# Attention of a two-block layer kernel: the values are multiplied with the probabilities as the stationary operand

## The chip, the cores and the metric

One Trainium2 chip, one of its cores. The metric is the device time of one launch in microseconds, median of several runs, lower is better.

## The reference, cut to what matters

Two layers run one after the other on 512 tokens of width 1024, all in float32. The change touches only the attention of the second layer and the norm behind it. There, eight heads "A" have three branches each (selected keys `slc`, a window `win`, compressed keys `cmp`), and eight heads "B" (`mla`) have one. With at most 16 blocks of 64 keys and 512 tokens the selection and the window cover every earlier key, so `slc`, `win` and `mla` are causal attention over 512 keys with value rows of width 64; `cmp` has 31 keys.

```python
o_c = einsum('bgrqn,bngd->bqgrd', masked_softmax(s_c, ...), vc)
o_s = einsum(...masked_softmax(s_s, mask_s)..., vs)
o_w = einsum(...masked_softmax(s_w, mask_w)..., vw)
o_a = gate0 * o_c + gate1 * o_s + gate2 * o_w          # 512 tokens x 8 heads x 64
o_b = einsum('bhqs,bshd->bqhd', masked_softmax(s), v)  # 512 tokens x 8 heads x 64
mixed = concat([rmsnorm(o_a, out_gain_a), rmsnorm(o_b, out_gain_b)]) @ w_out
h = x + mixed
return h + peer_ffn(rmsnorm(h, norm2_gain), ...)
```

## The kernel before, in words

Every engine has a program written out by hand, and semaphores join them. TensorE (PE) is the engine that nearly all of the work goes to.

The attention is a list of 104 steps, `STEPS`. A step is one branch of one head and one tile `qt` of 128 queries; it has `(qt+1)*128` keys. A head A has nine steps (`slc` 0, 1, `cmp`, `slc` 2, 3, `win` 0 to 3), so rounds 0 to 71 are the A heads; each B head has four, rounds 72 to 103. All engines go through the rounds `u` in the same order:

- PE, round `u`: `scores` of step `u+4` (L1076 to L1098, into PSUM bank `(u+4) % 4`), some products with values from `VALUES_AT[u]` (`output`, L1134; `cmp`: L1127), and `turn` of step `u` (L1108), which transposes the tiles of probabilities into PSUM bank `4 + u % 2`.
- VectorE (DVE), round `u`: `tops` of step `u` (row maximum of the scores, L2218) and `biases` (L2229); two rounds late `inverses` (L2242) and `shares` (L2257, L2259), which multiplies the whole tile of probabilities by one over its sum and by the gate. `turn` of the step waits for `shares`.
- ScalarE (ACT), round `u`: `probs` (Exp with its row sum, L1585), and `turned` of step `u-4`, which copies the transposed tiles out of PSUM (L1600). A head whose values are done is copied out as 64 rows (features) by 512 tokens (L1623) into `oall`.

In `output` the values (128 keys by 128 columns, of which a head uses 64) are stationary and the transposed probabilities move: for key tile `kt` there are `(4-kt)*128` columns. A float32 product is two instructions on PE. All branches of a head add up in one PSUM bank, so the result is feature by token.

The norm of `o_a` and `o_b`: GpSimd (POOL) squares and adds tiles of `oall` (L2609, L2613), PE sums over features with single columns (L1145), ACT takes the root (L1605) and needs the table of Sqrt in place of that of Exp for it, DVE inverts, PE spreads the root to rows (L1151), DVE scales (L2274), and POOL (heads A) or ACT and DVE (heads B) split the scaled tiles into a high and a low part (`a_parts`, `hh`, `hl`). The A part runs beside the B heads. Behind round 103 PE starts the output projection: `first_half(c)` is twelve products with the A part for output chunk `c`, `half_products(c, 1)` twelve with the B part (L689). Twenty-four of the 192 come ahead of the B norm's last PE work.

Of the kernel before, what the change touches and what calls it, by code (L numbers as in the profile page):

```python
# [15 lines left out]
P = 128  # L16
T = 512
# [190 lines left out]
def build(nc, xT_in, par_in, pT_in, cst_in, stream, pos_in, u_in, v_in, rows_in, out, dense, gelu):  # L208
    with ExitStack() as ctx:
# [25 lines left out]
        ptc = hnt  # L235
# [97 lines left out]
        pt = sb("pt", [P, 2, TT, T], c=two)  # L333
        st = sb("st", [P, 2, TT, 4], c=two)
        with ExitStack() as brief:
# [4 lines left out]
        sqo = sb("sqo", [P, 3, T], c=two)  # L340
# [66 lines left out]
        at_s, at_max, at_exp, at_scale, at_t, at_ev, at_pv, at_out = (  # L407
            sem(f"at_{v}") for v in ("scores", "max", "exp", "scale", "transposed", "evacuated", "pv", "out"))
# [28 lines left out]
        o_sum, o_row, o_ready, pool_order = (sem(v) for v in ("o_sum", "o_row", "o_ready", "pool_order"))  # L437
# [29 lines left out]
        vcz = [hnt[:, t // 3, (1 + t % 3) * P:(2 + t % 3) * P] for t in range(TT)]  # L467
# [5 lines left out]
        VALUES_AT = {}  # L473
        for h in range(A_H):
            for kt in range(TT):
                VALUES_AT.setdefault(PER * h + 6 + kt, []).append((3 * h + SLC, kt))
                VALUES_AT.setdefault(PER * h + 10 + kt, []).append((3 * h + WIN, kt))
            VALUES_AT[PER * h + 9].append((3 * h + CMP, 0))
        for n in range(3 * A_H, GN):
            for kt in range(TT):  # L480
                VALUES_AT.setdefault(STEP_OF[n, 0] + TT + 1 + kt, []).append((n, kt))
        VALUED = [n for u in sorted(VALUES_AT) for n, kt in VALUES_AT[u] if kt == TT - 1 or GROUPS[n][1] == "cmp"]
        HEAD_LAST = [3 * h + WIN for h in range(A_H)] + list(range(3 * A_H, GN))
        LAST_AT = {n: u for u in VALUES_AT for n, kt in VALUES_AT[u] if kt == TT - 1}

        def wide_of(n):
            return n % 2 if n >= 3 * A_H else n % 3
        LAG = 2
        COLUMN_A, ROW_A = NS - 6 * TT, NS - 4 * TT
        SCALED_A = [ROW_A + TT + k for k in (2, 4, 6, 8)]  # L490
# [4 lines left out]
        def cmp_state(n):  # L495
            at = R_MK + HEAD_OF[n] % 2 * 4 * TT
            return [rr[:, at + k * TT:at + (k + 1) * TT] for k in range(4)]
# [178 lines left out]
        def _(pe):  # L676
# [424 lines left out]
            def turn(n, qt):  # L1101

                u = STEP_OF[n, qt]
                pe.wait_ge(at_scale, u + 1)
                if u >= 2:
                    pe.wait_ge(at_ev, u - 1)
                for kt in range(1 if GROUPS[n][1] == "cmp" else qt + 1):
                    m = pe.transpose(ps[:, 4 + u % 2, kt * P:(kt + 1) * P], pr[:, u // TT % 2, u % TT, kt * P:(kt + 1) * P],  # L1108
                                     cc("ident"))
                m.then_inc(at_t, 1)  # L1110

            def output(n, kt):

                g, kind, at = GROUPS[n]
                head = HEAD_OF[n]
                bank = ps[:, 6 + head % 2, :]
                if kt == 0:
                    pe.wait_ge(at_ev, STEP_OF[n, 0 if kind == "cmp" else TT - 1] + 1)
                    if head >= 2 and kind != "win":
                        pe.wait_ge(at_out, head - 1)  # L1120
                if kind == "cmp":
                    if kt:
                        return
                    if head == 0:
                        pe.wait_ge(kr_copied, 2)
                    for t in range(TT):
                        m = pe.matmul(bank[:, t * P:(t + 1) * P], vcz[t], ptc[:, head % 2, 0:P], start=False, stop=False)  # L1127
                else:
                    if kind == "mla":
                        v = vm[:, kt, at // 2 * P:(at // 2 + 1) * P]  # L1130
                    else:
                        c = (kind == "win") * P
                        v = vtok[:, kt, c:c + P]
                    m = pe.matmul(bank[:, kt * P:], v, pt[:, wide_of(n), kt, kt * P:],  # L1134
                                  start=kind != "win" and kt == 0, stop=kind != "slc" and kt == TT - 1)
                if kind == "cmp" or kt == TT - 1:
                    m.then_inc(at_pv, 1)
# [4 lines left out]
            def o_column(rows):  # L1142

                for t in range(TT):
                    m = pe.matmul(ps[:, 0, P + t:P + t + 1], sqo[:, rows, t * P:(t + 1) * P], ones[:, 0:1], start=True, stop=True)  # L1145
                m.then_inc(sum_done, 1)

            def o_rows(parts, at=0):

                for t, part in enumerate(parts, at):  # L1150
                    m = pe.transpose(part, rn[:, 0, t:t + 1].to_broadcast([P, P]), cc("ident"))  # L1151
                m.then_inc(o_row, 1)

            for u in range(NS + TT + 1):
                if u == COLUMN_A:
                    pe.wait_ge(o_sum, 1)
                    pe.wait_ge(at_exp, u + 1)
                    o_column(0)
                elif u == ROW_A:
                    pe.wait_ge(inverse_done, 5)  # L1160
                    pe.wait_ge(at_exp, u + 1)
                    o_rows([ps[:, 0, (t + 1) * P:(t + 2) * P] for t in range(TT - 1)])
                elif u == ROW_A + 1:
                    pe.wait_ge(at_exp, u + 1)
                    o_rows([ps[:, 1, 2 * P:3 * P]], TT - 1)
                if u + TT < NS:
                    scores(*STEPS[u + TT])
                for n, kt in VALUES_AT.get(u, ()):
                    output(n, kt)
                if u < NS:  # L1170
                    turn(*STEPS[u])
            def half_products(c, half):

                rows = a_parts if half == 0 else [(hh[:, k, :], hl[:, k, :]) for k in range(4, DC)]
                at = 4 * half
                ready = None if c else (mix_low, DC + at)
                return split_products(3 + c % 4, out_w[c if c < 4 else c % 2], at * P, 4, P, lambda k: rows[k][0],
                                      lambda k: rows[k][1], half == 0, half == 1, ready)

            def first_half(c):  # L1180

                pe.wait_ge(x_add, X_BASE[U_OUT2] + c + 1)
# [3 lines left out]
            for c in range(4):  # L1186
                if c == 3:
                    pe.wait_ge(at_out, A_H + B_H - 1)
                first_half(c)
                if c == 0:  # L1190
                    pe.wait_ge(o_sum, 3)
                    o_column(1)
                elif c == 1:
                    pe.wait_ge(inverse_done, 6)
                    pe.wait_ge(at_out, A_H + B_H)
                    o_rows([ps[:, 7, t * P:(t + 1) * P] for t in range(TT)])
# [157 lines left out]
        def _(eng):  # L1354
# [215 lines left out]
            def probs(n, qt):  # L1570
# [4 lines left out]
                if u >= 2 * TT:  # L1575
                    eng.wait_ge(at_t, u - 2 * TT + 1)
                if GROUPS[n][1] == "cmp":
                    _, total, _, bias = cmp_state(n)
                    for t in range(TT):
# [6 lines left out]
                               accum_out=s_[:, 1:2]).then_inc(at_exp, 1)  # L1586

            def turned(n, qt):

                u, tok = STEP_OF[n, qt], slice(qt * P, (qt + 1) * P)  # L1590
                eng.wait_ge(at_t, u + 1)
                if GROUPS[n][1] == "cmp":
                    if n >= 6:
                        eng.wait_ge(at_pv, VALUED.index(n - 6) + 1)
                    eng.activation(ptc[:, HEAD_OF[n] % 2, 0:P], ps[:, 4 + u % 2, 0:P], ACT.Copy).then_inc(at_ev, 1)
                    return
                before = [m for m in range(n) if GROUPS[m][1] != "cmp" and wide_of(m) == wide_of(n)]
                if before:
                    eng.wait_ge(at_pv, VALUED.index(before[-1]) + 1)
                eng.activation(pt[:, wide_of(n), 0:qt + 1, tok],  # L1600
                               ps[:, 4 + u % 2, 0:(qt + 1) * P].rearrange("p (k q) -> p k q", q=P), ACT.Copy).then_inc(at_ev, 1)

            def o_inverse_root():

                eng.activation(rn[:, 0, :], ps[:, 0, P:P + TT], ACT.Sqrt, scale=1.0 / (A_H * A_D), bias=pc("eps")).then_inc(root_done, 1)  # L1605

            for u in range(NS + 2 * TT):
                if u == COLUMN_A + TT:
                    eng.wait_ge(sum_done, 21)
                    eng.wait_ge(at_max, u + 1)  # L1610
                    o_inverse_root()
                elif u == NS:
                    eng.activation(rn[:, 1, 1:2], zero[:, :], ACT.Sqrt)
                if u < NS:
                    probs(*STEPS[u])
                if TT <= u < NS + TT:
# [1244 lines left out]
```

## Time and profile before

| | |
|---|---|
| median of 3 runs | 2416.05 us (2415.91 to 2418.77) |
| the profiled execution | 2415.56 us, of which its span is 2413.6 us |
| PE busy | 2372.7 us, 98% |
| DVE, ACT, POOL busy | 1724.2, 838.4, 1114.0 us |
| attention | about 970 to 1138 us of the span |

Times in the views are microseconds from the start of the span. "Busy" is the time in which an engine had an instruction under way. A matmul's shown duration includes its way through the array, so the cost of one in a stream is read from start to start, not from its duration. PEld is the load of the stationary operand, which PE does beside its products.

### The profile page before, as it was taken

How to read it: one execution, taken by the hardware profiler on the slowest of the kernel's cores; microseconds unless marked ns; L12 is line 12 of the kernel's file. 1: busy time of each engine (PE TensorE's matmuls, PEld its weight loads, DVE VectorE, ACT ScalarE, POOL GpSimd, SP SyncE). 2: the span in 40 equal slices, each digit the busy share in tenths (PEclk: the TensorE clock that was granted, in tenths of full speed). 3: DMA queues.
4: the chain of work that ended last, by engine and by line, in shares of the span. 5: the costliest groups of instructions: out<-in, count | busy, mean ns of one | idle time of the engine just before them, and what ended most of it. 6: DMA issues, size and time to landing. Idle time of an engine off the chain costs nothing.

```text
span 2413.6 us, 35086 instructions
## 1 busy us (share of the span) xinstructions
PE 2372.7 (98%) x12248; PEld 2034.3 (84%) x12248; DVE 1724.2 (71%) x2873; ACT 838.4 (35%) x1445; POOL 1114.0 (46%) x747
## 2 busy tenths in 40 slices
PE   8999999999999999899999999999999999999999
PEld 6888888878888887666889999999999888888887
DVE  8888785463433656776637699798896788888887
ACT  4132222100113315776224333344443333333333
POOL 6777766665666550203563788731112322222220
PEclk9999999999999999899999999999999999999999
DMA  4333323433332223000124899899999999999995
GB/s 150 98 107 107 105 91 125 135 113 108 131 117 95 88 76 123 32 1 10 62 90 129 276 312 307 295 356 341 345 343 400 385 354 352 351 358 350 353 356 200
DMA packets 181333, 490.41 MB, mean 203 GB/s; under 512 B 14848, under 2 KB 80512, under 8 KB 181248
## 3 DMA queue, kind: packets, MB, share of 16 engines
q1 hardware_dynamic: 144384, 355.12, 43.6%
q0 software_dynamic: 36864, 134.23, 15.0%
q8 instruction: 44, 0.72, 0.1%
q14 instruction: 41, 0.34, 0.0%
HBM read 436.86 MB, written 52.43 MB: 203 GB/s over the span
## 4 chain that ended last, share of the span: by engine, by line
PE 89%; issue 3%; POOL 3%; DVE 2%; ACT 1%; DMA 0%; SPq 0%; DVEq 0%; POOLq 0%; ACTq 0%
PE ps L689 40%; PE ps L1295 22%; PE ps L1255 17%; POOL spl L2657 2%; PE ps L1276 2%; PE ps L1134 2%; PE ps L1108 1%; POOL rare L2667 1%; PE ps L873 1%; PE ps L1047 1%; PE ps L993 1%; PE ps L1093 0%; DVE st L2218 0%; PE ps L794 0%; PE ps L893 0%
## 5 line engine op out<-in xcount | busy, mean ns | idle before, releaser
L1255 PE MATMUL ps<-hh,spl 128*128 128x384 f32 x2048 | 535.3, 337 | 2.9 <-POOL spl L2657 2.9
L689 PE MATMUL ps<-hh,spl 128*128 128x512 f32 x1728 | 535.3, 389 | 1.5 <-DVE x L1934 0.8
L1295 PE MATMUL ps<-spl,wsp 128*128 128x512 f32 x2304 | 523.8, 389 | 0.0
L1295 PEld LDWEIGHTS ps<-spl,wsp 128*128 128x128 f32 x2304 | 432.0, 188 | 89.4
L1647 ACT ACTIVATE spl<-ring 128x1024 fp32r<-128x1024 f32 x256 | 271.7, 1061 | 677.1 <-PE ps L1255 330.4
L2530 POOL TENSOR_TENSOR spl<-ring,spl 128x1024 fp32r<-128x1024 f32 (+1 forms) x164 | 427.4, 2606 | 13.1
L689 PEld LDWEIGHTS ps<-hh,spl 128*128 128x128 f32 x1728 | 324.3, 188 | 69.5 <-DVE x L1934 1.2
L1255 PEld LDWEIGHTS ps<-hh,spl 128*128 128x128 f32 x2048 | 371.1, 188 | 6.1 <-issue 5.4
L2528 POOL CAST spl<-ring 128x1024 fp32r<-128x1024 f32 (+1 forms) x164 | 186.3, 1136 | 355.3 <-PE ps L689 335.3
L1255 PE MATMUL ps<-hl,spl 128*128 128x384 f32 x1024 | 342.5, 334 | 0.0
L2429 DVE TENSOR_TENSOR spl<-ring,spl 128x1024 fp32r<-128x1024 f32 x192 | 235.2, 1225 | 147.7 <-ACT spl L1647 136.3
L689 PE MATMUL ps<-hl,spl 128*128 128x512 f32 x864 | 336.2, 389 | 0.0
L2676 POOL DMA_INDIRECT rare<-v_in,rstd x128 | 125.5, 980 | 394.2 <-DVE ps L2491 365.4
L2667 POOL DMA_INDIRECT rare<-rows_in,rstd x128 | 127.6, 997 | 230.1 <-DVE rare L2358 214.6
L1255 PEld LDWEIGHTS ps<-hl,spl 128*128 128x128 f32 x1024 | 192.5, 188 | 0.0
L689 PEld LDWEIGHTS ps<-hl,spl 128*128 128x128 f32 x864 | 162.2, 188 | 33.7
L2657 POOL TENSOR_TENSOR spl<-ring,spl 128x1024 fp32r<-128x1024 f32 x64 | 153.7, 2401 | 74.0 <-ACT spl L1647 73.6
L2358 DVE SCALAR_TENSOR_TENSOR rare<-rare,ps 128x1024 f32<-128x1024 f32 x128 | 150.4, 1217 | 21.5 <-DMA rare<-rows_in,rstd 21.1
L2491 DVE SCALAR_TENSOR_TENSOR ps<-rare,rstd,ps 128x1024 f32<-128x1024 f32 x128 | 164.2, 1283 | 1.7 <-PE ps L1305 1.7
L689 PE MATMUL ps<-acth,spl 128*128 128x512 f32 x352 | 109.0, 390 | 2.5 <-DVEq L1980 1.7
L689 PE MATMUL ps<-hu,spl 128*128 128x512 f32 x256 | 81.1, 392 | 0.0
L689 PEld LDWEIGHTS ps<-acth,spl 128*128 128x128 f32 x352 | 66.1, 188 | 17.0 <-issue 3.3
(451 smaller groups left out, 3405.2 us busy)
## 6 DMA issues: line engine op xcount, KB each, us to landing
ring<-stream_in SPq DMA_DIRECT2D x134, 512.0 KB
ring<-u_in SPq DMA_DIRECT2D x128, 512.0 KB
ring<-v_in SPq DMA_DIRECT2D x128, 512.0 KB
ring<-stream_in SPq DMA_DIRECT2D x60, 704.0 KB
gelu<-gst SPq DMA_DIRECT2D x128, 192.0 KB
dense<-stage SPq DMA_DIRECT2D x12, 2048.0 KB
gl<-gelu SPq DMA_DIRECT2D x32, 768.0 KB, 7.0
gw<-dense SPq DMA_DIRECT2D x32, 768.0 KB, 9.7
```

The source lines that it names most:

```text
L689: m = pe.matmul(ps[:, bank, :], w[:, part, k0 + k * n:k0 + k * n + P], rhs(k), start=first and k == 0 and part == 0 and rhs is high, stop= ...
L1255: m = pe.matmul(ps[:, bank, 0:TD], w[:, part, k0 + k * P:k0 + (k + 1) * P], rhs(k), start=first and k == 0 and part == 0 and rhs is high, ...
L1295: m = pe.matmul(ps[:, bank, :], wsp[:, j % 2, part, tok], spl[:, j % 2, row, cols], start=False, stop=last and n == 2)
L1647: eng.activation(spl[:, j % 2, 0, 0:D], ring[:, j % RING, 0:D], ACT.Copy).then_inc(hi_done, 1)
L2358: dve.scalar_tensor_tensor(out=rows_of[row], in0=rows_of[row], scalar=1.0, in1=xt, op0=ALU.mult, op1=ALU.mult, accum_out=dots[:, one_at(at ...
L2429: dve.tensor_tensor(spl[:, at % 2, 1, 0:D], ring[:, at % RING, 0:D], spl[:, at % 2, 0, 0:D].bitcast(F32), ALU.subtract).then_inc(lo_done, 1)
L2491: dve.scalar_tensor_tensor(out=acc, in0=rows_of[s % ROW_SLOTS], scalar=dots[:, one_at(i * 16 + s)], in1=acc, op0=ALU.mult, op1=ALU.add).th ...
L2528: pool.tensor_copy(w[:, 0, 0:n], ring[:, j, 0:n]).then_inc(wt_high, 1)
L2530: pool.tensor_tensor(w[:, 1, 0:n], ring[:, j, 0:n], w[:, 0, 0:n].bitcast(F32), ALU.subtract).then_inc(wt_low, 1)
L2657: pool.tensor_tensor(spl[:, j % 2, 1, 0:D], ring[:, j, 0:D], spl[:, j % 2, 0, 0:D].bitcast(F32), ALU.subtract).then_inc(lo_done, 1)
L2667: pool.indirect_dma_start(rows_of[s % ROW_SLOTS], None, rows_in, bass.IndirectOffsetOnAxis(place[:, s:s + 1], 0))\
L2676: pool.indirect_dma_start(rows_of[s % ROW_SLOTS], None, v_in.rearrange("b a d -> (b a) d"), bass.IndirectOffsetOnAxis(place[:, s:s + 1], 0 ...
```

## The change

- The product with values is turned round: the transposed probabilities are stationary and the 64 value columns of the head move. `values(u)` does one step: for each key tile `kt <= qt` one product of 128x128 by 64, into its own 64 columns of PSUM, so the result is token by feature. `cmp` is one product of 256 moving columns (values laid out in blocks, `vcz`).
- The shares (one over the sum, times the gate) are no longer put on the probabilities: `weigh_head` on DVE multiplies the result, 128 tokens by 4 tiles by 64, once for each head and branch, eight rounds behind the last step of it, and adds the branches. `turn` waits for `probs` alone.
- The copies of transposed tiles are done by DVE for `cmp` and for `qt` 0 and 1 (`evacuate_turned`, in DVE's round `u+5`) and by ACT for `qt` 2 and 3 (in ACT's round `u+2`). The 64-row copies of heads are gone.
- The norm's sums are row sums: ACT squares with an accumulator. PE turns the token-major result with the identity scaled by the inverse root (`turned_by`): `turned_chunk`, four products of 128 columns for each of eight chunks. Four are put into rounds 85, 89, 93 and 97, where each takes a place in the two PSUM banks of the transposes (`turn_slot`), and four behind the loop. ACT makes the high part from PSUM (`part_high`), DVE the low part (`part_low`; for the first four in DVE's round `at + 6`). POOL's work on norms and parts is gone.
- `first_half(0)` comes ahead of the values of the last step, `first_half(1)` and `(2)` behind them, and then the four last turned chunks and `first_half(3)`.

```diff
+        TURN_LAG, VALUE_LAG, WEIGH_LAG = 2, 3, 8
+        A_SQUARES, A_ROOT = A_H * PER + 6, A_H * PER + 10
+        A_TURNS = [A_H * PER + 13 + 4 * k for k in range(TT)]
+        def turn_slot(u, chunk=False):
+            return u + chunk + sum(at < u for at in A_TURNS)
+        def slot_user(k):
+            for c, at in enumerate(A_TURNS):
+                if turn_slot(at, True) == k:
+                    return mix_low, DC + c + 1
+            return evacuated(next(u for u in range(NS) if turn_slot(u) == k))
...
-                pe.wait_ge(at_scale, u + 1)
                 if u >= 2:
-                    pe.wait_ge(at_ev, u - 1)
+                    pe.wait_ge(*slot_user(turn_slot(u) - 2))
...
-                    m = pe.matmul(bank[:, kt * P:], v, pt[:, wide_of(n), kt, kt * P:], ...)
+                    for kt in range(qt + 1):
+                        m = pe.matmul(out_[:, qt, :], turned[:, kt * P:(kt + 1) * P], v, start=kt == 0, stop=kt == qt)
...
+            def turned_chunk(c, bank):
+                for t in range(TT):
+                    m = pe.matmul(ps[:, bank, t * P:(t + 1) * P], oall[:, c // TT * TT + t, c % TT * P:(c % TT + 1) * P],
+                                  turned_by[:, t, :], start=True, stop=True)
+            for u in range(NS):
+                pe.wait_ge(at_exp, u + 1)
+                if u + TT < NS:
+                    scores(*STEPS[u + TT])
+                if u >= VALUE_LAG:
+                    values(u - VALUE_LAG)
+                turn(u)
+                if u in A_TURNS:
+                    c = A_TURNS.index(u)
+                    if c == 0:
+                        pe.wait_ge(inverse_done, 5)
+                    pe.wait_ge(*slot_user(turn_slot(u, True) - 2))
+                    turned_chunk(c, turn_bank(u, True))
+            values(NS - 3)
+            values(NS - 2)
+            first_half(0)
+            values(NS - 1)
+            first_half(1)
+            first_half(2)
+            pe.wait_ge(inverse_done, 6)
+            for c, bank in zip(range(TT, DC), (0, 5, 6, 7)):
+                turned_chunk(c, bank)
+            first_half(3)
...
+            for u in range(NS + WEIGH_LAG - 1):          # DVE
                 if u < NS:
                     top = step.mark(tops(*STEPS[u]))
+                if 0 <= u - TT - 1 < NS and on_dve(u - TT - 1):
+                    evacuate_turned(u - TT - 1)
                 if u < NS:
                     step.meet(top)
                     biases(*STEPS[u])
+                for n in END_AT.get(u - WEIGH_LAG, ()):
+                    weigh_head(n)
+                if u == A_INVERSE:
                     o_inverted(1)
+                elif u - TT - 2 in A_TURNS:
+                    c = A_TURNS.index(u - TT - 2)
+                    part_low(c, turn_bank(u - TT - 2, True), a_parts[c][1], a_parts[c][0])
```

## Rows read from the trace of the kernel before

**Rows 1.** The page's first part: busy time, share of the span, instructions

```profile
PE 2372.7 (98%) x12248; PEld 2034.3 (84%) x12248; DVE 1724.2 (71%) x2873; ACT 838.4 (35%) x1445; POOL 1114.0 (46%) x747
```

**Rows 2.** Windows: length, PE, PEld, DVE, ACT, POOL busy (instructions), clock, DMA

```profile
974.60:985.66 11.06, 8.32 (x35) 6.25 (x36) 9.68 (x34) 8.26 (x30) 2.15 (x1) 0.55 0.27 90
985.82:1065.04 79.22, 72.34 (x471) 54.54 (x470) 60.53 (x234) 62.34 (x204) 10.53 (x15) 1.00 0.03 8
985.66:1127.15 141.49, 130.71 (x786) 93.67 (x785) 106.57 (x393) 107.26 (x332) 26.95 (x38) 1.00 0.03 9
```

**Rows 3.** Waits in 985.82:1065.04 (six heads A): us in total, times, longest

```profile
PE ps L1134 <- ACT pt L1600: 6.9, 6, 1.3
```

**Rows 4.** PE groups by form, 974 to 1138 us: busy us, mean ns, idle before

```profile
L1134 PE MATMUL ps<-pt,vtok 128*128 128x512 f32 x32 | 17.7, 633 | 8.0 <-ACT pt L1600 8.0
...
L1127 PE MATMUL ps<-hnt 128*128 128x128 f32 x64 | 8.5, 275 | 0.0
...
L1134 PE MATMUL ps<-pt,vtok 128*128 128x128 f32 x32 | 7.0, 301 | 0.0
```

**Rows 5.** Timeline, PE: start us, length of the run, count of instructions

```profile
946.67 14.40 PE L1047 MATMUL ps<-blk,ring 128*128 128x62 f32 x128
...
1012.05 0.97 PE L1087 MATMUL ps<-kcz,kq 128*128 128x31 f32 x8
...
1016.11 1.06 PE L1127 MATMUL ps<-hnt 128*128 128x128 f32 x8
```

**Rows 6.** Windows around the last fall of the clock, columns as in rows 2

```profile
956.00:960.00 4.00, 4.00 (x38) 4.00 (x38) 0.00 (x0) 0.22 (x1) 0.00 (x0) 1.00 0.84 282
968.00:970.00 2.00, 0.77 (x6) 0.41 (x4) 1.80 (x7) 0.00 (x0) 0.18 (x1) 1.00 0.00 0
```

**Rows 7.** Timeline, DVE: single operations at five places

```profile
977.78 0.18 DVE L2240 RECIPROCAL rr<-rr 128x4 f32<-128x4 f32 x1
...
1024.02 0.54 DVE L2259 TENSOR_SCALAR pr<-pr,st,vtok 128x512 f32<-128x512 f32 x1
...
1102.26 0.69 DVE L2218 TENSOR_REDUCE st<-ps 128x1 f32<-128x512 f32 x1 [1.27 <-PE ps L1098]
...
1104.34 0.42 DVE L2218 TENSOR_REDUCE st<-ps 128x1 f32<-128x256 f32 x1
...
1111.48 0.28 DVE L2284 COPY rstd<-ps 128x128 f32<-128x128 f32 x1
...
1113.90 0.74 DVE L2274 SCALAR_TENSOR_TENSOR oall<-oall,par,rstd 128x512 f32<-128x512 f32 x1
```

**Rows 8.** Timeline, PE: from round 99 into the projection

```profile
1127.15 1.02 PE L1093 MATMUL ps<-mqk 96*128 96x512 f32 x2
...
1128.08 0.65 PE L1134 MATMUL ps<-pt,vm 128*128 128x256 f32 x2
1128.56 0.60 PE L1108 MATMUL ps<-cst,pr 128*128 128x128 f32 x4
...
1137.85 1.86 PE L689 MATMUL ps<-oah,spl 128*128 128x512 f32 x7
...
1140.70 0.95 PE L1145 MATMUL ps<-cst,sqo 128*128 128x1 f32 x8
...
1144.34 0.60 PE L1151 MATMUL ps<-cst,rn 128*128 128x128 f32 x4
```

**Rows 9.** Timeline, ACT: the two table loads around the A root, one Exp

```profile
1097.05 1.28 ACT L1605 ACT_TABLE_LOAD   x1
...
1098.63 1.28 ACT L1585 ACT_TABLE_LOAD   x1
...
1129.67 0.78 ACT L1585 ACTIVATE pr<-ps,st,rr 128x512 f32<-128x512 f32 x1 [0.84 <-DVE st L2229]
```

**Rows 10.** Timeline at the start of the loop: DVE's first long wait, PE's first transpose

```profile
971.23 2.07 DVE L2229 TENSOR_TENSOR st<-st,rr 128x1 f32<-128x1 f32 x1
...
974.60 0.48 PE L1108 MATMUL ps<-cst,pr 128*128 128x128 f32 x1 [0.63 <-DVE pr L2259]
```

More of the change, by code:

```diff
@@ L482, in build @@
[L482 to L490, printed above, removed]
+        ENDS = [(h * PER + 4, (3 * h + CMP, 3 * h + SLC)) for h in range(A_H)]
@@ new lines, in build @@
+        ENDS += [(h * PER + 8, (3 * h + WIN,)) for h in range(A_H)]
+        ENDS += [(A_H * PER + (h + 1) * TT - 1, (3 * A_H + h,)) for h in range(B_H)]
+        END_AT = dict(sorted(ENDS))
+        WEIGHED = {n: k + 1 for k, n in enumerate(n for heads_ in END_AT.values() for n in heads_)}
+        BANK_OF = {n: 6 + (GROUPS[n][1] == "win" if n < 3 * A_H else n % 2) for n in range(GN)}
+        END_OF = {n: u for u, heads_ in END_AT.items() for n in heads_}
+        BANK_FREE = {n: max((WEIGHED[m] for m in range(GN) if BANK_OF[m] == BANK_OF[n] and END_OF[m] < END_OF[n]), default=0)
+                     for n in range(GN)}
@@ new lines, in build, with on_dve, evacuated, region @@
+        A_DONE, B_DONE = 3 * A_H, GN
+        def on_dve(u):
+            return GROUPS[STEPS[u][0]][1] == "cmp" or STEPS[u][1] < 2
+        def evacuated(u):
+            mine = sum(on_dve(w) == on_dve(u) for w in range(u + 1))
+            return (at_ev_dve if on_dve(u) else at_ev_act), mine
+        def region(n):
+            at = (GROUPS[n][1] == "cmp") * TT * A_D
+            return ps[:, BANK_OF[n], at:at + TT * A_D].rearrange("p (t d) -> p t d", t=TT)
+        def head_rows(n):
+            head = HEAD_OF[n]
+            half, at = divmod(head, A_H)
+            return oall[:, half * TT:(half + 1) * TT, at * A_D:(at + 1) * A_D]
@@ L492, in keys_of, with turn_bank @@
+        def turn_bank(u, chunk=False):
+            return 4 + turn_slot(u, chunk) % 2
+        A_INVERSE = A_H * PER + 14
+        B_EARLY = 6
+        NORM_SUMS = [rr[:, R_MK + k * TT:R_MK + (k + 1) * TT] for k in range(3)]
         def keys_of(n, qt):
@@ L496, in cmp_state @@
             at = R_MK + HEAD_OF[n] % 2 * 4 * TT
-            return [rr[:, at + k * TT:at + (k + 1) * TT] for k in range(4)]
+            return [rr[:, at + k * TT:at + (k + 1) * TT] for k in range(2)]
         def root_of(n, qt):
@@ L1109, in turn, with values @@
                                      cc("ident"))
                 m.then_inc(at_t, 1)
-            def output(n, kt):
+            def values(u):
+                n, qt = STEPS[u]
                 g, kind, at = GROUPS[n]
[L1115 to L1120, printed above, removed]
+                out_, turned = region(n), pt[:, u % TT, :]
+                pe.wait_ge(*evacuated(u))
+                if qt == 0 and BANK_FREE[n]:
+                    pe.wait_ge(at_weighed, BANK_FREE[n])
@@ L1121, in output @@
                 if kind == "cmp":
-                    if kt:
-                        return
-                    if head == 0:
+                    if HEAD_OF[n] == 0:
                         pe.wait_ge(kr_copied, 2)
-                    for t in range(TT):
-                        m = pe.matmul(bank[:, t * P:(t + 1) * P], vcz[t], ptc[:, head % 2, 0:P], start=False, stop=False)
-                else:
[L1129 to L1135, printed above, removed]
@@ L1136, in output @@
-                if kind == "cmp" or kt == TT - 1:
-                    m.then_inc(at_pv, 1)
+                    m = pe.matmul(out_, turned[:, 0:P], vcz[:, :, g * A_D:(g + 1) * A_D], start=True, stop=True)
+                else:
+                    for kt in range(qt + 1):
+                        if kind == "mla":
+                            v = vm[:, kt, at * B_V:(at + 1) * B_V]
+                        else:
+                            c = (kind == "win") * P + g * A_D
+                            v = vtok[:, kt, c:c + A_D]
+                        m = pe.matmul(out_[:, qt, :], turned[:, kt * P:(kt + 1) * P], v, start=kt == 0, stop=kt == qt)
@@ L1141, in _ @@
                 scores(*STEPS[u])
[L1142 to L1171, printed above, removed]
             def half_products(c, half):
@@ L1585, in probs, with turned @@
                 eng.activation(pr[:, u // TT % 2, u % TT, 0:nk], ps[:, u % TT, 0:nk], ACT.Exp, bias=s_[:, 3:4], scale=root_of(n, qt),
-                               accum_out=s_[:, 1:2]).then_inc(at_exp, 1)
-            def turned(n, qt):
-                u, tok = STEP_OF[n, qt], slice(qt * P, (qt + 1) * P)
+                               accum_out=total[:, qt:qt + 1]).then_inc(at_exp, 1)
+            def turned(u):
+                n, qt = STEPS[u]
                 eng.wait_ge(at_t, u + 1)
[L1592 to L1613, printed above, removed]
+                if u >= TT:
+                    eng.wait_ge(at_pv, u - TT + 1)
@@ L1614, in _, with part_high @@
+            def part_high(c, bank, row):
+                eng.wait_ge(o_turned, c + 1)
+                eng.activation(row, ps[:, bank, :], ACT.Copy, scale=pc("out_gain", at=c)).then_inc(mix_high, 1)
+            early = B_EARLY * A_D
+            for u in range(NS + TURN_LAG):
                 if u < NS:
                     probs(*STEPS[u])
-                if TT <= u < NS + TT:
-                    turned(*STEPS[u - TT])
-                for head, n in enumerate(HEAD_LAST):
-                    if u != LAST_AT[n] + 3:
-                        continue
-                    rows = slice(head % 2 * A_D, (head % 2 + 1) * A_D)
-                    eng.wait_ge(at_pv, VALUED.index(n) + 1)
-                    eng.activation(oall[rows, head // 2, :], ps[rows, 6 + head % 2, :], ACT.Copy).then_inc(at_out, 1)
@@ L1624, in _ @@
-            eng.wait_ge(at_out, A_H + B_H)
-            eng.wait_ge(sum_done, 22)
-            o_inverse_root()
-            for c in range(4, DC):
-                eng.wait_ge(o_ready, c + 1)
-                eng.activation(hh[:, c, :], oall[:, c, :], ACT.Copy).then_inc(mix_high, 1)
+                if u >= TURN_LAG and not on_dve(u - TURN_LAG):
+                    turned(u - TURN_LAG)
+                if A_SQUARES <= u < A_SQUARES + TT:
+                    eng.wait_ge(at_weighed, A_DONE)
+                    o_squares_of(u - A_SQUARES, 0, T)
+                elif u == A_ROOT:
+                    eng.wait_ge(o_squares, TT)
+                    o_inverse_root(NORM_SUMS[0])
+                elif u - 2 in A_TURNS:
+                    c = A_TURNS.index(u - 2)
+                    part_high(c, turn_bank(u - 2, True), a_parts[c][0])
+                elif u >= NS - 2:
+                    eng.wait_ge(at_weighed, A_DONE + B_EARLY)
+                    o_squares_of(TT + u - (NS - 2), 0, early)
@@ L1630, in _ @@
+            eng.activation(rn[:, 1, 1:2], zero[:, :], ACT.Sqrt)
+            eng.wait_ge(at_weighed, B_DONE)
+            for t in range(TT):
+                o_squares_of(2 * TT + t, early, T, t * P)
+            eng.wait_ge(o_sum, 1)
+            o_inverse_root(NORM_SUMS[1])
+            for c, bank in zip(range(TT, DC), (0, 5, 6, 7)):
+                part_high(c, bank, hh[:, c, :])
             raw_parts(7, X_BASE[U_OUT2] + 4, "norm2", hu)
@@ L2244, in shares, with weigh_head @@
-            def shares(n, qt):
+            def weigh_head(n):
                 g, kind, at = GROUPS[n]
-                u = STEP_OF[n, qt]
-                col = 2 * P + (g * A_R + at) * 3 + ("cmp", "slc", "win").index(kind) if kind != "mla" else 0
+                total, part = totals[:, 0, n % 8, :], totals[:, 1, n % 8, :]
+                out_, tmp = head_rows(n), weighted[:, WEIGHED[n] % 2, :, :]
+                every_column = part.unsqueeze(2).to_broadcast([P, TT, A_D])
+                dve.wait_ge(at_exp, END_OF[n] + 1)
@@ L2249, in shares @@
                 if kind == "cmp":
-                    _, _, part, _ = cmp_state(n)
+                    step(dve.tensor_scalar(total, total, 1e-20, None, ALU.max))
+                step(dve.reciprocal(part, total))
+                if kind != "mla":
+                    col = 2 * P + (g * A_R + at) * 3 + ("cmp", "slc", "win").index(kind)
                     step(dve.tensor_tensor(part, part, vtok[:, :, col:col + 1].rearrange("p t c -> p (t c)"), ALU.mult))
-                    p_ = pr[:, u // TT % 2, u % TT, 0:P].rearrange("p (t n) -> p t n", t=TT)[:, :, 0:N_CMP]
@@ L2260, in shares, with evacuate_turned @@
-                o.then_inc(at_scale, 1)
+                dve.wait_ge(at_pv, END_OF[n] + 1)
+                if kind in ("cmp", "mla"):
+                    dve.tensor_tensor(out_, region(n), every_column, ALU.mult).then_inc(at_weighed, 1)
+                else:
+                    step(dve.tensor_tensor(tmp, region(n), every_column, ALU.mult))
+                    dve.wait_ge(at_weighed, WEIGHED[n] - 1)
+                    dve.tensor_tensor(out_, out_, tmp, ALU.add).then_inc(at_weighed, 1)
+            def evacuate_turned(u):
+                n, qt = STEPS[u]
+                nk = P if GROUPS[n][1] == "cmp" else keys_of(n, qt)
+                dve.wait_ge(at_t, u + 1)
+                if u >= TT:
+                    dve.wait_ge(at_pv, u - TT + 1)
+                dve.tensor_copy(pt[:, u % TT, 0:nk], ps[:, turn_bank(u), 0:nk]).then_inc(at_ev_dve, 1)
```

173 lines of the change are left out of this document (56 added, 117 removed).

## The prediction, made before the changed kernel was run

> **What bounds the kernel now.** I read the page first: PE is busy in 98% of the span [rows 1], and the chain that ended last runs over PE nearly everywhere, so a microsecond that PE loses or gains in the attention arrives at the end. I then cut windows around the attention. From round 7 (985.66) to round 99 (1127.15) PE is busy 130.7 of 141.5 us [rows 2]; six heads A take 79.22 us, 13.2 us each, with 72.34 us busy, 12.06 us a head [rows 2]. The idle rest of 1.15 us a head is, by the waits, one wait per head of a product with values for the copy of transposed probabilities on ACT: 6.9 us in six times [rows 3]. DVE is busy 76% and ACT 79% of that stretch [rows 2], so neither is the bound. So there are two things to price: how many microseconds PE's own work changes, and which waits go and come.
>
> **PE's work: products with values.** Before, a branch has four products with 512, 384, 256 and 128 moving columns, two instructions each. Between the forms of 512 and 128 columns lie 332 ns for 384 columns [rows 4], 0.865 ns a column, so a branch costs 2 x 1280 x 0.865 = 2.2 us. After, it has ten products of 64 columns, twenty instructions, each with a 128x128 load of its own. No row has exactly that form, but three stand around it: 128 instructions with 62 moving columns took 14.40 us, 0.1125 us each; eight with 31 columns 0.97 us and eight with 128 columns 1.06 us, which, less the 0.275 us that one takes by itself [rows 4], is 0.10 and 0.11 each [rows 5]. Whether 31, 62 or 128 columns move, one goes out every 0.11 us: the load sets the pace and the 64 columns (0.055 us) lie beside it. Twenty make 2.25 us. So turning the product round saves nothing in itself: the unused half of the columns is gone, but now the loads set the pace. `cmp` goes from eight instructions (0.89 us) to two of 256 columns (0.44 us). A head A: 2 x 0.05 - 0.45 = -0.35 us, to 11.7 us.
>
> There is a rule that speaks against this: the Trainium skill, "TensorE: Matmul & The Clock Gate", Part 3, The mechanism, says that a load overlaps products in flight only where it goes to another group of rows of the array; all loads here use all rows. By it the moving columns would add to each load (0.11 + 0.055 us), which is my third rival. The trace disagrees: with 128 moving columns, 0.11 us of moving by themselves, the pace was still 0.11 us [rows 5]. The sum goes by the rows.
>
> **Waits that go.** `turn` no longer waits for `shares` (0.54 us at 512 columns [rows 7]) two DVE rounds late, and `values(u)` is three rounds behind a copy that needs only `turn`. I walked through one head with 11.7 us of PE work in nine unequal rounds (0.9 to 2.1 us). ACT loses the copies of small tiles and of heads, so its copies come 0.5 us or more ahead of need. The one tight place is DVE's round 3 of each head, where the shares of `slc` and `cmp` of the head before are made together: seven small operations at about 0.2 us from start to start [rows 7], two products out of PSUM at 0.42 us (the nearest row is the 256-column reduction [rows 7]), one addition, some 2.2 us. The copies for `turn` of the rounds 2 and 3 stand behind it and come 0 to 0.6 us late; I take 0.25 us. A head A then takes 11.95 us in place of 13.2. Rounds 7 to 71 are 7.2 heads: **-9.0 us**. Bounds: no wait left, -11; all of the 1.15 us back, -2.5.
>
> **The B heads, rounds 72 to 98.** Before they take 141.5 - 7.2 x 13.2 = 46.5 us, norm of A and its waits included. After: scores 1280 columns twice, at 0.93 us from start to next start for 512 with the causal product [rows 8], 2.4 us a head; ten transposes at 0.11, 1.1; values 2.25; together about 5.8 us, times 6.75 heads 39.2 us. To this come:
> - four turned chunks of eight instructions with 128 columns, at 0.89 us each by [rows 5]: 3.55 us that PE did not have;
> - the root of A: two table loads of 1.28 us and the root [rows 9] stop ACT for 2.8 us as before, and four squares before it, about 0.7 us each by the nearest row, the Exp of 512 columns at 0.78 [rows 9], use up its lead. From its lead of about 1 us in my walk 1.7 us of waiting are left on PE (before: 2.0);
> - the new wait. The chunk of round 85 sits in slot 86, and `turn(87)` has slot 88, so it waits for that chunk's `part_low`. DVE does it in its round 91, which begins with `tops(91)`, and the scores of step 91 are only issued in PE's round 87, just ahead. All of that round stands on PE's path: reduction of 512 columns 0.69, bias, as small as the others, 0.2, then `weigh_head` of a B head (0.18 + gap + 0.42 = 0.7), then `part_low` 0.74 [rows 7]. With the gaps the slot is free 2.4 us after the end of the scores; PE has only `values(84)`, 0.22 us, to do, and behind `turn(87)` the next scores stand in its queue. Idle about 2.25 us, and the same in rounds 91, 95 and 99, since all lie four apart. Three fall here: 6.75 us; 0.3 us for `turn(86)`, which is now only one place behind `turn(85)` in the banks.
>
> Sum 39.2 + 3.55 + 1.7 + 7.05 = 51.5 us: **+5.0 us**. Bounds: no new wait, -2; waits of 3 us, +7.5.
>
> **Both ends.** At the start PE waits for DVE, whose bias stands 2.07 us behind POOL's split of weights [rows 10]; POOL's work stays, so `turn(0)` comes 0.85 us earlier (at once behind the scores of round 0) but round 3 does not, and for most of that stretch the clock is at its lower level of 1.2 GHz (0.55 on average [rows 2]); now three steps' values lie in this slow stretch too. I keep round 7 at 985.3: **-0.4 us** (bounds -3 and +2).
> At the end, before: round 99 at 1127.15, first product of the projection at 1137.85, and inside it 0.8 us of column sums and 0.55 us of rows spread again [rows 8]: 12.1 us beside the 192 products. After, from round 99: scores 0.93, wait for the fourth `part_low` 2.25, `values(96)` 0.22, transposes 0.44; then ACT, which stood behind `turn(99)`, has two more Exps, squares of 0.6 and an Exp of 0.78 [rows 9], until PE gets through round 103, about 7.2 us from the start of round 99; `values(101)`, `(102)` with a small wait 1.3; `first_half(0)` covers the last copy; `values(103)` 0.89. The norm's chain behind it (share 0.5, four squares 1.8, root, inverse, four scaled identities, 4.4 us) lies under two first halves (5.5 us at 0.23 us a product [rows 8]). Four chunks 3.55. About 12.9 us: **+0.8 us**. That POOL no longer squares and splits costs and gives nothing of its own; its two weight splits wait for heads as before. The parts of the B chunks lie under `first_half(3)`.
>
> **Sum**: -9.0 + 5.0 - 0.4 + 0.8 = -3.6 us. From the profiled 2415.56 us (span 2413.6 and 2.0 around it) 2412.0; the median of the runs is 0.5 us above the profiled one, so 2412.5 us. A measurement of this kernel tells about 0.2%, 4.8 us, from no change.
>
> **Rivals.**
> 1. *The new wait isn't there or is covered*: DVE has finished its round in time because PE is late anyway. Then only the work decides: four times 2.25 us less, 2403.5. Against it: the scores that DVE's round needs are issued by PE two instructions ahead of the wait, so no lead of DVE can help.
> 2. *DVE's double share stops PE in each head A* (the slower side). If round 3 on DVE takes 3.5 us in place of 2.2, since each of its small operations waits for the one before, `turn(2)` and `turn(3)` stand about 1.3 us later in each of eight heads: +9 us, 2421.5. It decides from about 2.6 us on; from 3.3 us on the kernel is slower than before. The pieces at 0.2 us [rows 7] speak against it; that DVE and ACT show waits in turn already, for it.
> 3. *Loads don't overlap the columns* (the rule above): 24 branches x 20 x 0.055 = +26 us, 2438. The rows speak against it.
> 4. *The clock falls*. With 64 columns the array streams half the time. In 946 to 961, with 62 columns, it stayed at 1.00, 2.4 GHz, and fell behind 970 after a stretch with PE busy 0.77 of 2 us [rows 6]. At 1.2 GHz over the A heads: 2450 or more.
>
> **Chances.** Forecast (both the new wait and a nearly full PE in the A heads) 0.48; its own range is 2408 to 2417, about a third of it below the bound of 2411.2. Rival 1 0.26. Rival 2 0.16. Rivals 3 and 4 and the unforeseen 0.10. Faster by over 0.2%: 0.26 + 0.16 = 0.42; slower: half of rival 2, and the 0.10, with a little of the forecast, 0.20; within: 0.38. The range for 8 in 10 goes from rival 1 to rival 2: 2402 to 2423.
>
> **What will show it.** Right: the group of products with values x480 (beside the x16 of `cmp`) at a pace of 0.11 us; period of a head A near 12.0 us (start to start of the x8 `cmp` scores); four PE waits of about 2.2 us in rounds 87, 91, 95, 99, released by DVE's low part; clock 1.00 from about 985 on. Wrong: a period above 12.7 us with PE waiting for DVE's copies; no long waits in the B rounds; a pace near 0.165 us. What would make it wrong is above all a queue effect of the kind that I could only walk through.

## The result and the profile after

The changed kernel takes 2420.98 us (median of 20 runs, 2418.66 to 2424.93) against 2415.81 us of the kernel before (20 runs): a ratio of 1.0018, 95% interval 1.0012 to 1.0025. It is 5.2 us slower; 3.6 us faster was forecast. The profiled execution took 2421.1 us, with a span of 2419.2.

| | before | forecast | after |
|---|---|---|---|
| a head A | 13.2 us | 11.95 | 11.5 |
| round 7 begins | 985.66 | 985.3 | 985.78 |
| PE waits for `part_low` in rounds 87, 91, 95, 99 | - | 2.25 us each | 1.96 us each |
| PE wait behind the root of A | 1.41 us | 1.7 | 1.62 |
| round 99 begins | 1127.15 | 1122.8 | 1127.02 |
| stretches at 1.2 GHz behind round 72 | none | none | 20.4 us |

The timeline of PE after, from the A heads to the projection (start us, length of the run, instructions, idle before it):

```profile
985.78 0.98 PE L1124 MATMUL ps<-kcz,kq 128*128 128x31 f32 x8
...
997.29 0.98 PE L1124 MATMUL ps<-kcz,oah 128*128 128x31 f32 x8
...
1084.52 1.05 PE L1167 MATMUL ps<-vm,pt 128*128 128x64 f32 x8
1085.40 0.50 PE L1144 MATMUL ps<-cst,pr 128*128 128x128 f32 x3
1087.53 1.10 PE L1130 MATMUL ps<-mqk 96*128 96x512 f32 x2 [1.62 <-ACT pr L1613]
...
1097.96 0.66 PE L1144 MATMUL ps<-cst,pr 128*128 128x128 f32 x4 [1.96 <-DVE oah L2315]
...
1107.16 0.92 PE L1144 MATMUL ps<-cst,pr 128*128 128x128 f32 x4 [1.96 <-DVE oah L2315]
...
1119.54 0.65 PE L1144 MATMUL ps<-cst,pr 128*128 128x128 f32 x4 [1.96 <-DVE il L2315]
...
1130.29 0.66 PE L1144 MATMUL ps<-cst,pr 128*128 128x128 f32 x4 [1.96 <-DVE il L2315]
...
1136.29 2.23 PE L1167 MATMUL ps<-vm,pt 128*128 128x64 f32 x10
1138.28 3.33 PE L726 MATMUL ps<-oah,spl 128*128 128x512 f32 x7
```

The idle time before a line stands in brackets, with what ended it. The first two lines are one period of a head A, 11.51 us. The next two show the pace of the new products with values: eight instructions in 0.88 us, 0.11 us each. The four waits for `part_low` (DVE L2315) are there, at the places named. The second of them and the last line show what was not forecast: four transposes take 0.92 us where the first wait has 0.66, and seven products of the projection 3.33 us where [rows 8] have 1.86. The granted clock explains it. Windows, columns as in [rows 2]. The first is seven heads A, the next four are cut from one 512-column score product of the B heads to the next, and the last goes from round 99 to the four last turned chunks:

```profile
985.78:1066.27 80.49, 80.49 (x672) 71.67 (x671) 65.02 (x251) 59.26 (x194) 3.82 (x5) 1.00 0.03 8
1087.53:1094.69 7.16, 7.07 (x51) 5.73 (x51) 3.36 (x12) 4.36 (x13) 0.00 (x0) 1.00 0.00 0
1094.69:1103.89 9.20, 7.15 (x52) 5.73 (x51) 4.12 (x13) 4.18 (x11) 0.00 (x0) 1.00 0.01 2
1103.89:1116.28 12.39, 10.34 (x53) 8.65 (x52) 4.12 (x13) 4.18 (x11) 0.00 (x0) 0.72 0.00 0
1116.28:1127.02 10.74, 8.69 (x52) 7.16 (x51) 4.12 (x13) 4.18 (x11) 0.00 (x0) 0.84 0.01 2
1127.02:1149.01 21.99, 20.03 (x95) 17.45 (x94) 4.97 (x17) 9.22 (x29) 0.00 (x0) 0.77 0.01 1
```

In the A heads PE is busy 80.49 of 80.49 us, seven heads without one wait, and the clock is at 1.00 (2.4 GHz). Three windows of a B head with a chunk have the same work and the same wait, yet take 9.20 us at clock 1.00, 12.39 at 0.72 and 10.74 at 0.84. In windows of 1 us the clock is at 1.00 or at 0.50 except where it changes, so a mean of 0.72 over 12.39 us is 6.9 us at 1.2 GHz, 0.84 over 10.74 is 3.4, and 0.77 over 21.99 is 10.1: together 20.4 us. Taken against the first of them, the first low stretch costs 12.39 - 9.20 = 3.2 us, the second 1.5; the third is priced below.

### The profile page after: what moved, and what is told of

Same layout as the page of the kernel before. It is cut to its first block, busy times and chain, and to the rows that moved or that the text cites. A ratio compares the mean times of both kernels' runs of the same rounds, so it can differ in the third digit from the quotient of the medians.

```text
span 2419.2 us, 35569 instructions
## 1 busy us (share of the span) xinstructions
PE 2383.1 (99%) x12528; PEld 2064.6 (85%) x12528; DVE 1708.6 (71%) x2818; ACT 824.9 (34%) x1401; POOL 1088.5 (45%) x711
## 4 chain that ended last, share of the span: by engine, by line
PE 91%; POOL 3%; issue 3%; DVE 2%; ACT 1%; DMA 0%; SPq 0%; DVEq 0%; POOLq 0%; ACTq 0%
PE ps L726 40%; PE ps L1320 22%; PE ps L1280 17%; POOL spl L2652 2%; PE ps L1167 2%; PE ps L1301 2%; PE ps L1144 1%; POOL rare L2662 1%; PE ps L1130 1%; PE ps L910 1%; PE ps L1084 1%; PE ps L1030 1%; PE ps L1133 0%; PE ps L1134 0%; PE ps L831 0%
```

## The experiments

Each time is the median of 5 or more runs. The ratios are against the kernel before, run beside it on the same chip.

**early_low: take the wait away.** `part_low` of a chunk moves from the end of DVE's round `at + 6` to the end of round `at + 5`, ahead of the round whose scores PE has only just issued. Nothing else changes.

```diff
-                elif u - TT - 2 in A_TURNS:
-                    c = A_TURNS.index(u - TT - 2)
-                    part_low(c, turn_bank(u - TT - 2, True), a_parts[c][1], a_parts[c][0])
+                elif u - TT - 1 in A_TURNS:
+                    c = A_TURNS.index(u - TT - 1)
+                    part_low(c, turn_bank(u - TT - 1, True), a_parts[c][1], a_parts[c][0])
```

> DVE's part_low of a chunk one round earlier (at + 5), before the round that waits for scores just issued. All theories: the four PE waits of 1.96 us go, 7.8 us less. Theory idle (the waits made TensorE's clock fall): no stretch at 0.50 in the B rounds any more, the fall behind round 99 shorter or gone; 2404 to 2408 us. Theory narrow (products of 64 columns alone made it fall): the falls stay though nothing waits; 2411 to 2415 us.

Measured: 2403.4 us (2401.7 to 2408.41), ratio to before 0.9945 (0.9932 to 0.9959). Windows of the profiled execution, three B heads and then the stretch from round 99 to the turned chunks of B:

```profile
1099.95:1121.04 21.09, 20.83 (x152) 16.97 (x151) 12.07 (x40) 12.53 (x33) 0.00 (x0) 1.00 0.01 2
1121.04:1136.38 15.34, 15.34 (x95) 12.98 (x94) 4.51 (x17) 9.00 (x29) 0.00 (x0) 1.00 0.01 2
```

A B head now takes 7.03 us, against 9.20 for the same with the wait at full clock, and the second window does the 95 PE instructions of the last window of the changed kernel in 15.34 us, not 21.99. Of this difference of 6.65 us, 1.96 are the wait; the other 4.7 us are what the third low stretch cost. So the low stretches cost 3.2 + 1.5 + 4.7 = 9.4 us and the waits 4 x 1.96 = 7.8 us, 17.2 us together; the kernel became 17.6 us faster. This profiled execution was the slowest of its five (2408.41 us). It has one low stretch of its own, just behind the 1.62 us wait for the root of A:

```profile
1088.00:1091.50 3.50, 1.88 (x12) 1.31 (x12) 1.45 (x5) 2.86 (x8) 0.00 (x0) 0.99 0.00 0
1091.50:1098.30 6.80, 6.80 (x29) 5.77 (x29) 1.76 (x9) 2.86 (x7) 0.00 (x0) 0.51 0.00 0
```

The four other runs, 2401.7 to 2404.7 us, granted 0.997 on average over their spans against 0.995 of this one. The changed kernel had the same wait of 1.62 us, and its clock stayed at 1.00 behind it. So a wait of 1.6 us is followed by a low stretch in some executions and in others not.

**wide_b: keep the waits, move 128 columns.** The products with values of the B heads take both heads of the pair, 128 columns, into a bank of their own, and DVE reads the half that belongs to the head.

```diff
-                            v = vm[:, kt, at * B_V:(at + 1) * B_V]
+                            v = vm[:, kt, at // 2 * P:(at // 2 + 1) * P]
...
+                made = region(n)[:, :, at % 2 * B_V:(at % 2 + 1) * B_V] if kind == "mla" else region(n)
...
-                    dve.tensor_tensor(out_, region(n), every_column, ALU.mult).then_inc(at_weighed, 1)
+                    dve.tensor_tensor(out_, made, every_column, ALU.mult).then_inc(at_weighed, 1)
```

> The B heads' products with values move 128 columns (both heads of the pair, one half unused), at the same number of instructions; the four waits stay. Loads set the pace, so no time is added by the columns themselves. Theory narrow: the clock stays at 1.00 in rounds 72 to 103; about 2412 us. Theory idle: the same falls as in the changed kernel; 2420 to 2422 us. If columns and loads were not beside each other: 2430 us.

Measured: 2415.0 us (11 runs, 2413.79 to 2416.62), ratio to before 0.9996 (0.9987 to 1.0005), 6 us below the changed kernel, with the same waits (1.90 to 1.91 us). Neither theory's expectation held: the falls are fewer but not gone. Three B heads with a chunk and its wait, and the stretch behind them:

```profile
1094.76:1104.01 9.25, 7.30 (x53) 5.82 (x51) 4.12 (x13) 4.18 (x11) 0.00 (x0) 1.00 0.01 2
1104.01:1114.79 10.78, 8.84 (x52) 7.20 (x51) 4.12 (x13) 4.18 (x11) 0.00 (x0) 0.84 0.00 0
1114.79:1124.04 9.25, 7.31 (x53) 5.83 (x52) 4.11 (x13) 4.18 (x11) 0.00 (x0) 1.00 0.01 2
1124.04:1142.97 18.93, 17.03 (x95) 14.82 (x94) 4.97 (x17) 9.10 (x29) 0.00 (x0) 0.91 0.00 1
```

A mean of 0.84 over 10.78 us and one of 0.91 over 18.93 are 3.4 us at 1.2 GHz each, 6.8 us together against 20.4. The other runs agree: all 11 of wide_b granted 0.995 or 0.996 on average over the span, the 20 of the changed kernel 0.991 to 0.994. A head takes 9.25 us against 9.20: twice the columns cost 0.05 us in 20 instructions.

**early_wide: both edits.**

> Both edits. Both theories: no falls in the B rounds, 2404 us. If either early_low or wide_b alone has the clock at 1.00 throughout, this is equal to early_low within 2 us.

Measured: 2401.99 us (2401.75 to 2403.46), 0.9941 (0.9928 to 0.9955). Equal to early_low within 2 us. Its runs spread over 1.7 us, those of early_low over 6.7, and the profiled one has no low stretch in the B rounds.

**before_held: the waits without the change.** To see whether waits alone do it, the kernel before, with its 128 to 512 moving columns, gets four waits in the same rounds: `turn` of rounds 87, 91, 95, 99 waits for later shares, and DVE makes two reductions that nobody uses ahead of them.

```diff
+        HELD = (87, 91, 95, 99)
...
-                pe.wait_ge(at_scale, u + 1)
+                pe.wait_ge(at_scale, u + (3 if u in HELD else 1))
...
+                if u - TT in HELD:
+                    for k in (2, 3):
+                        dve.tensor_reduce(rn[:, 1, k:k + 1], x[:, 0, :], AX_X, ALU.max)
```

> The kernel before, whose values move 128 to 512 columns, with four waits put in: turn of rounds 87, 91, 95 and 99 waits for the shares made in DVE's round four later, and DVE has two reductions of 512 numbers that nobody uses ahead of them, about 2.2 us of idle PE each. Theory both (the fall needs long waits and narrow products together): no stretch at 0.50 behind round 72, and the waits alone cost 6 to 9 us, 2422 to 2425 us. Theory idle (waits alone are enough): falls behind rounds 91 to 99 as in the changed kernel, 2428 us or more.

Measured: 2428.64 us (2425.68 to 2431.54), 1.0052 (1.0038 to 1.0066). Waits of 1.94, 1.94, 3.49 and 1.94 us, 9.3 us in all; the kernel became 13.0 us slower (the runs beside it took 2415.63), so something beside the waits costs 3.7 us. Windows around the second to the fourth, which end at 1121.50, 1132.75 and 1142.32:

```profile
1116.00:1120.00 4.00, 3.56 (x16) 1.87 (x14) 3.50 (x13) 2.23 (x7) 0.00 (x0) 1.00 0.02 4
1120.00:1124.00 4.00, 2.50 (x14) 2.13 (x14) 2.92 (x8) 2.44 (x6) 0.26 (x1) 0.79 0.00 0
1124.00:1128.00 4.00, 4.00 (x15) 2.08 (x14) 2.36 (x7) 1.37 (x6) 3.78 (x6) 0.78 0.00 0
1128.00:1132.00 4.00, 1.26 (x5) 0.40 (x3) 4.00 (x8) 1.90 (x5) 3.84 (x7) 1.00 0.00 0
1132.00:1136.00 4.00, 3.25 (x14) 2.82 (x15) 2.18 (x7) 1.73 (x7) 1.30 (x3) 0.57 0.00 0
1136.00:1140.00 4.00, 4.00 (x19) 2.20 (x17) 2.56 (x9) 2.23 (x8) 2.19 (x3) 1.00 0.00 0
1140.00:1144.00 4.00, 2.02 (x10) 1.24 (x9) 3.31 (x10) 1.79 (x4) 0.00 (x0) 0.85 0.00 0
```

The clock falls here too, at the end of the third wait and behind the second and the fourth. Narrow products are not needed for it; the theory that both are needed together fell. What they seem to do is lengthen it: 10.2 us at 1.2 GHz here, 20.4 in the changed kernel with shorter waits. The single stretches say the same. With 128 or more moving columns all six in the traces last 3.4 us (three here, two in wide_b, one in early_wide_act); with 64, five of seven last 6.8 or 10.2 us (three stretches in the changed kernel, three in act_copies, one in early_low).

**before_lag2: one line of the kernel before.** A head A lost its 1.15 us wait. Was that the turned product, or only where the copy stands in ACT's order? This is the kernel before, with ACT copying step `u-2` in its round `u`, not `u-4`.

```diff
-                if TT <= u < NS + TT:
-                    turned(*STEPS[u - TT])
+                if 2 <= u < NS + 2:
+                    turned(*STEPS[u - 2])
```

> The kernel before with one edit: ACT copies the transposed tiles of step u-2 in its round u, not u-4. Theory lag (the one wait per head A was the late place of the copy in ACT's order): the waits of products with values for the copy go, a head A takes 12.1 in place of 13.2 us, 2407 us. Theory product (the wait goes only with the new product, which can start on a tile alone, and with transposes that don't wait for the shares): 2414 to 2420 us, ACT now stands behind transposes.

Measured: 2403.54 us (2402.48 to 2406.46), 0.9953 (0.994 to 0.9967): 12.3 us faster than before with one line. Six heads A, columns as in [rows 2], and then the stretch ahead of round 7, in the kernel before and here:

```profile
983.10:1055.52 72.42, 72.31 (x470) 54.54 (x469) 57.66 (x235) 60.62 (x204) 8.12 (x11) 1.00 0.03 9
...
970.00:985.66 15.66, 12.30 (x56) 9.17 (x56) 13.81 (x43) 9.74 (x34) 6.59 (x4) 0.56 0.21 67
...
970.00:983.10 13.10, 11.25 (x53) 8.38 (x53) 12.53 (x39) 8.41 (x29) 6.32 (x4) 0.61 0.25 81
```

PE is as busy as before (72.3 us [rows 2]), and the 6.9 us of [rows 3] are gone; a head A takes 12.07 us. Round 7 begins at 983.10, 2.6 us earlier. These two are 7.2 x 1.13 + 2.6 = 10.7 of the 12.3 us; the rest is in the B heads. But of the 2.6 us about 1.8 are clock: by the means, 10.2 us ahead of round 7 are at 1.2 GHz in place of 13.8. One profiled execution each doesn't show whether the edit shortened that stretch. What the edit surely brings is the 8.1 us of the A heads.

**act_copies, early_act: all copies on ACT.** `on_dve(u)` gives False for every step, first in the changed kernel, then in early_low.

> All copies of transposed tiles on ACT again, DVE has none; the rest as in the changed kernel. My walk through a head: ACT gets 1.3 us of copies more per head A (8.0 to 9.3 of 11.5 us), the copies come later and PE waits 0 to 0.5 us a head: 2421 to 2425 us. Rival: the split of the copies is what took the wait from the A heads: period back at 12.5 us or more, 2428 us or more.

Measured: 2417.45 us (10 runs, 2411.05 to 2422.8), 1.0004 (0.9994 to 1.0013), 3.5 us below the changed kernel, where 0 to 4 us above had been expected. My walk had PE waiting up to 0.5 us a head for ACT's copies, but a head A takes 11.4 us with them, 0.1 less than with DVE's. The four waits and 20.5 us at 1.2 GHz are there as in the changed kernel.

> part_low one round earlier and all copies on ACT. If the 3.5 us that act_copies was below the changed kernel come from the start of the loop and the heads A, they add to early_low: 2400 us. If they came from fewer low-clock stretches there, nothing adds: 2403 us.

Measured: 2398.46 us (2397.0 to 2405.05), 0.9933 (0.992 to 0.9947), the lowest median of the set, 4.9 us below early_low. Windows: six heads A, then three B heads with a chunk; below them the stretch ahead of round 7, in the changed kernel and here:

```profile
982.05:1050.50 68.45, 68.45 (x579) 61.05 (x578) 51.68 (x186) 57.11 (x199) 3.83 (x5) 1.00 0.03 9
1090.02:1109.96 19.94, 19.94 (x152) 16.67 (x151) 11.04 (x34) 14.19 (x39) 0.00 (x0) 1.00 0.01 2
...
970.00:985.78 15.78, 14.07 (x67) 11.39 (x68) 11.11 (x28) 8.32 (x28) 6.72 (x4) 0.57 0.21 68
...
970.00:982.05 12.05, 11.21 (x65) 8.98 (x65) 10.25 (x23) 8.10 (x29) 6.36 (x4) 0.72 0.28 88
```

A B head with a chunk takes 6.65 us, against 7.03 in early_low: DVE's copy of step 85 came late for `turn(86)`, by 0.25 us, and so behind each of the four chunks; the forecast has 0.3 us once. With four such heads, 0.1 us in seven A heads and a start that is some 3 us earlier, the difference is about accounted for. The start is a matter of the clock: 6.7 us ahead of round 7 are at 1.2 GHz in place of 13.6, which is 3.4 of the 3.7 us by which round 7 begins earlier than in the changed kernel. With all copies on ACT this stretch is 6.8 us in one profiled execution and 10.2 in four; with copies on DVE it is 10.2 in one and 13.6 in three. That the place of the copies decides it isn't shown.

**early_wide_act, root_later, act_root_later.** Wide products with the copies on ACT, and the root of A in round 84 in place of 82, with 128 and with 64 columns.

```diff
-        A_SQUARES, A_ROOT = A_H * PER + 6, A_H * PER + 10
+        A_SQUARES, A_ROOT = A_H * PER + 6, A_H * PER + 12
```

> The same with 128 moving columns in the B heads. 1 to 2 us below early_act if some of its runs still have a low stretch behind the root of A, with a smaller spread: 2398.5 us.

> The same with the root of A (two table loads on ACT) in round 84 in place of 82. If the 1.6 us that PE waits there depend on how short the following rounds of PE are: 0.5 to 1.5 us less than early_wide_act; if ACT's lead is the same in every round: equal within 0.5 us, or slower where the first chunk then waits for the inverse root.

> early_act (part_low one round earlier, all copies on ACT, 64 columns) with the root of A in round 84. As with 128 columns the later root saves 1.3 us: 2397.2 us, the best of the set. If the 1.3 us were only fewer low stretches: 2398.5 us.

Measured, in this order: 2401.88 us (2401.39 to 2404.11; 0.9944, 0.9931 to 0.9958); 2400.57 (2398.87 to 2402.68; 0.9937, 0.9923 to 0.995); 2398.77 (2398.54 to 2402.56; 0.9937, 0.9924 to 0.9951). With the chunks' waits gone and all copies on ACT, 128 columns are 2 to 3 us slower than 64 by the medians, not faster, though the runs overlap: a B head takes 6.83 us against 6.65, 1.4 us over eight heads, and the profiled execution has a low stretch of 3.4 us. With the later root the median is 1.3 us lower with 128 columns and 0.3 us higher with 64, and its wait is still there (1.7 and 1.8 us). So the move is not worth making.

## Why the prediction was wrong

**PE's own work in the A heads was right.** The twenty instructions of 64 columns of a branch go at the pace of their loads. PE's work in a head A was put at 11.7 us; the changed kernel does a head in 11.5 with PE busy throughout. Had the columns been added to each load, as rival 3 has it, 64 more columns would have cost about 0.055 us in each of 20 instructions, 1.1 us a head. Doubling them cost 0.05 us a head in wide_b and 0.18 at most (6.83 against 6.65). The Trainium skill, "TensorE: Matmul & The Clock Gate", Part 3, The mechanism, says that a load overlaps products in flight only where it goes to another group of rows of the array, and names a background weight buffer as another way. The runs disagree with the first for these products, whose loads use all rows; no run tells whether the second is what happens here.

**The A heads were right in kind**: the wait went and nothing came for it. The size was 9.0 us less by the forecast and 7.2 x 1.7 = 12.2 us less as measured; the double share on DVE, my rival 2, delayed next to nothing (0.1 us a head against act_copies, where 0.25 was in the sum). But the reason was only half seen. The forecast gave it to the turned product and to shares that no longer stand ahead of the transposes; before_lag2 shows that the place of the copy in ACT's order is enough to take the whole wait away, at 12.07 us a head. What is left for all the rest of the change is 12.07 to 11.5 us, 0.57 us, where the forecast had 0.35 us of PE work.

**The new wait was right**, in its four places, its releaser and nearly its size (1.96 for 2.25 us). Rival 1 fell. The wait behind the root was right too (1.62 for 1.7), though the wait that it was set beside was 1.4 us and not 2.0 in the kernel before:

```profile
1100.79 0.52 PE L1108 MATMUL ps<-cst,pr 128*128 128x128 f32 x3 [1.41 <-ACT pt L1600]
```

The rest of PE's work in the B heads was put too low: a head with a chunk takes 9.20 - 1.96 = 7.24 us at full clock, where 5.8 + 0.89 = 6.7 were in the sum. The late `turn(86)` was seen, but it comes behind every chunk.

**The step that failed** is the refusal of rival 4, that the clock falls, and the line "clock 1.00 from about 985 on" that followed from refusing it. The clock did fall, not in the A heads, where the rival had put it, but in the B heads behind the waits that the forecast itself had found. It was judged by [rows 5] and [rows 6], 14 us of 62-column products with PE never idle; that shows narrow products to be harmless by themselves, which the A heads confirm. [rows 6] also show that the clock fell after PE had been busy 0.77 of 2 us, and this was not set beside four waits of 2 us that were just being put into the sum. So the clock stood at nothing in the sum, and a term of +9.4 us was missing. early_low shows it: the waits away, the low stretches behind them went too, and the kernel gained 17.6 us, not 7.8.

That 2421.0 - 9.4 = 2411.6 us lies 0.9 from the forecast of 2412.5 is in part luck. Beside the clock, the A heads gave 3.2 us more than forecast, while the B heads cost 2.3 us more (rounds 7 to 99 are 0.2 us shorter than before, so the B heads are 12.0 us longer, 4.7 of them by the clock; 7.3 for 5.0) and round 7 began 0.5 us later; these errors cancel.

**What stays open.** Which waits bring a fall. In the traces of the changed kernel, act_copies, wide_b and before_held, the first of the four waits is followed by none, the second and the fourth by one in all four, the third by one in all but wide_b; the 1.6 us wait behind the root is followed by one in some executions; in the kernel before, waits of up to 1.6 us in the B rounds are followed by none. The traces don't say whether it is the idle time of one wait, of several together, or their place in time. That narrow products lengthen the low stretches rests on seven stretches against six, and on the 6 us and the mean clocks between the runs of the changed kernel and wide_b; why they do was not tried.

## What to carry to other kernels

A new wait on PE can cost more than its length: here four waits of 2 us cost 7.8 us themselves and 9.4 us in clock, so the stretch behind each new wait is priced at 1.2 GHz too, as a case of its own. And before a rewrite takes the credit for a wait that goes, move the one instruction that is waited for by itself: one line of order gave 12.3 us here, as much as the whole rewrite once its own wait was mended (early_low, 12.3 us against the runs beside it). Its best form, early_act, is 5 us below that one line.

## What was not expected of the hardware

With four idle stretches of 1.9 to 2.0 us (one of 3.5 us in before_held), 8 to 12 us apart, the granted clock fell to its lower level for 3.4 to 10 us at a time, with 64 columns moving (20.4 us in all), with 128 (6.8 us) and with 128 to 512 (10.2 us). With no idle stretch it stayed at 1.00 through 80 us of A heads, whose products with values move 64 columns. A B head with its chunk lost 3.2 us in a low stretch of 6.9 us, nearly half of it.
